# Products with gathered V rows in tiles of 32 columns, four tokens side by side

## The reference, cut to what matters

```
def gathered_attention(q, k_sel, v_sel, valid):
    logits = jnp.einsum('thd,tkhd->thk', q, k_sel).astype(jnp.float32) * (HEAD_DIM ** -0.5)
    logits = jnp.where(valid[:, None, :], logits, -jnp.inf)
    p = jax.nn.softmax(logits, axis=-1).astype(v_sel.dtype)
    return jnp.einsum('thk,tkhd->thd', p, v_sel)
```

## Time and profile before

| | |
|---|---|
| median of the runs | 1961.01 us |
| the profiled execution's own time | 1973.61 us |
| its span | 1971.5 us |
| mean granted TensorE clock | 0.905 |
| PE busy | 1653.0 us (84%) |
| DVE busy | 1057.1 us (54%) |
| ACT busy | 441.1 us (22%) |
| POOL busy | 582.4 us (30%) |

### The profile page before, as it was taken

The page is one execution under the profiler, slowest core; times in us unless marked ns, Lnnn a source line. Parts: engine busy times, 40 slices in busy tenths (PEclk is TensorE's granted clock), DMA queues, the critical chain, the costliest instruction groups (busy, mean ns, idle before and its releaser), DMA issues.

```text
span 1971.5 us, 23185 instructions
## 1 busy us (share of the span) xinstructions
PE 1653.0 (84%) x8977; PEld 1295.0 (66%) x8977; DVE 1057.1 (54%) x1778; ACT 441.1 (22%) x681; POOL 582.4 (30%) x435
## 2 busy tenths in 40 slices
PE   4875899889999699946966957776787999999998
PEld 1222388668888476846863532222786999999998
DVE  0516099988652338384888977842544333333223
ACT  2311322112112333211212320002112333322110
POOL 4001034324433222316775527774500000000000
PEclk8997999889999888988985569999898999999999
DMA  9894023222222122315997725664321222222222
GB/s 254 301 350 153 9 78 99 70 73 88 86 86 81 40 81 63 84 50 197 350 309 237 227 68 166 175 196 151 112 75 43 75 80 80 85 85 74 76 80 85
DMA packets 156032, 249.85 MB, mean 127 GB/s; under 512 B 11431, under 2 KB 104359, under 8 KB 155693
## 3 DMA queue, kind: packets, MB, share of 16 engines
q1 hardware_dynamic: 129296, 160.13, 25.6%
q0 software_dynamic: 24592, 81.40, 13.5%
q10 hardware_dynamic: 2069, 7.34, 1.1%
HBM read 238.39 MB, written 10.79 MB: 126 GB/s over the span
## 4 chain that ended last, share of the span: by engine, by line
PE 60%; DVE 19%; DMA 7%; POOL 7%; issue 4%; ACT 3%; SPq 0%; DVEq 0%; ACTq 0%; POOLq 0%
PE ps L410 32%; PE ps L452 12%; POOL kv L1964 6%; DVE EQ L1509 3%; DMA ring<-w_ffn_in 3%; PE ps L575 2%; DVE G L1739 2%; DVE kprod L1736 2%; PE ps L440 1%; PE ps L737 1%; PE ps L739 1%; PE ps L738 1%; PE ps L794 1%; PE ps L713 1%; DMA ring<-w_ffn_out 1%
## 5 line engine op out<-in xcount | busy, mean ns | idle before, releaser
L1880 POOL TENSOR_TENSOR w_lo<-w_raw,w_hi 128x1024 fp32r<-128x1024 f32 (+1 forms) x106 | 252.9, 2388 | 468.6 <-ACT w_hi L916 468.5
L916 ACT ACTIVATE w_hi<-w_raw 128x1024 fp32r<-128x1024 f32 (+1 forms) x192 | 198.4, 1034 | 803.4 <-PE ps L410 389.1
L410 PE MATMUL ps<-h_hi,w_hi 128*128 128x288 f32 x1088 | 236.8, 300 | 65.4 <-POOL w_lo L1880 25.6
L1230 DVE TENSOR_TENSOR w_lo<-w_raw,w_hi 128x1024 fp32r<-128x1024 f32 x86 | 103.2, 1201 | 271.5 <-ACT w_hi L916 265.4
L410 PE MATMUL ps<-h_lo,w_hi 128*128 128x288 f32 x1088 | 234.7, 298 | 0.0
L410 PE MATMUL ps<-h_hi,w_lo 128*128 128x288 f32 x1088 | 234.5, 297 | 0.0
L410 PEld LDWEIGHTS ps<-h_hi,w_hi 128*128 128x128 f32 x1088 | 177.1, 191 | 69.5 <-issue 23.4
L410 PEld LDWEIGHTS ps<-h_lo,w_hi 128*128 128x128 f32 x1088 | 177.3, 191 | 0.0
L410 PEld LDWEIGHTS ps<-h_hi,w_lo 128*128 128x128 f32 x1088 | 177.0, 191 | 0.0
L853 PE MATMUL ps<-kv,zq 128*128 128x512 f32 x256 | 131.3, 645 | 39.0 <-DMA kv<-cache_v,idxT 37.1
L1964 POOL DMA_INDIRECT kv<-cache_k,idxT x128 | 136.0, 1063 | 79.8 <-DVE kprod L1736 52.1
(11 more groups left out here) (427 smaller groups left out, 2873.1 us busy)
## 6 DMA issues: line engine op xcount, KB each, us to landing
w_raw<-w_ffn_in SPq DMA_DIRECT2D x88, 512.0 KB, 3.5
ring<-w_ffn_in SPq DMA_DIRECT2D x44, 512.0 KB, 7.8
w_raw<-w_ffn_out SPq DMA_DIRECT2D x40, 512.0 KB, 3.4
w_raw<-w_in SPq DMA_DIRECT2D x36, 512.0 KB, 3.7
qb<-q_scratch SPq DMA_DIRECT2D x64, 256.0 KB, 4.9
ring<-w_ffn_out SPq DMA_DIRECT2D x22, 512.0 KB, 6.9
ring<-w_in SPq DMA_DIRECT2D x12, 512.0 KB, 6.2
gate_scratch<-sgb ACTq DMA_DIRECT2D x8, 576.0 KB, 6.5
```

What stands on the lines that cost most here:

```text
L410: mm = pe.matmul(ps[:, 4 * half + 2 * m + hf_, 0:HALF], w[:, k, m * P:(m + 1) * P], x[:, kc0 + k, hf_ * HALF:(hf_ + 1) * HALF], start=(fir ...
L916: act.activation(w_hi[:, slot, 0:n], w_raw[:, slot, 0:n], ACT.Copy).then_inc(S_("hi_ready"), 1)
L1230: dve.tensor_tensor(w_lo[:, slot, 0:n], w_raw[:, slot, 0:n], w_hi[:, slot, 0:n].bitcast(F32), ALU.subtract)\
L1880: pool.tensor_tensor(w_lo[:, slot, 0:n], w_raw[:, slot, 0:n], w_hi[:, slot, 0:n].bitcast(F32), ALU.subtract)\
```

## The change

PE takes the tokens of a group in four rounds of four. The 128 output columns are divided into four tiles of 32. In round r, token a of the four goes into tile a (PSUM partitions 32a to 32a + 31), with its 8 live columns at 8r within the tile. In a round PE first issues the first half (c=0) of all four tokens, each behind the waits for its rows and its zq, and then the second half of all four; `pv_used` is added to after each token's second half. Loops over tokens are written out on PE and ACT. So that partition 8t of the bank still belongs to token t of the group, POOL and ACT take the tokens in the order that `value_token` gives: buffer a holds in round r the token 4a + r of the group. K is gathered in the old order. The number of DMAs, of products and of buffers stays the same.

```diff
+        def value_token(n):
+
+            return 16 * (n // 16) + 4 * (n % 4) + n % 16 // 4
...
-            with pe.Fori(0, 4) as g:
-                for qi in range(16):
-                    j = qi % 4
-                    pe.wait_ge(S_(f"kv_in{j}"), 32 * (16 + 4 * g + qi // 4 + 1))
-                    pe.wait_ge(S_("zq_ready"), 16 * g + (qi + 1))
-                    if qi == 0:
+            for g in range(4):
+                for r in range(4):
+                    if r == 0:
                         pe.wait_ge(S_("mz_ready"), g + 1)
                     for c in range(2):
-                        mm = pe.matmul(ps[:, 0, :], zq[:, j, c, 120 - 8 * qi:248 - 8 * qi], kv[:, j, c, :],
-                                       start=(qi == 0 and c == 0), stop=(qi == 15 and c == 1))
-                    mm.then_inc(S_("pv_used"), 1)
+                        for a in range(4):
+                            if c == 0:
+                                pe.wait_ge(S_(f"kv_in{a}"), 32 * (16 + 4 * g + r + 1))
+                                pe.wait_ge(S_("zq_ready"), 16 * g + 4 * r + a + 1)
+                            mm = pe.matmul(ps[32 * a:32 * a + 32, 0, :], zq[:, a, c, 24 - 8 * r:56 - 8 * r], kv[:, a, c, :],
+                                           start=(r == 0 and c == 0), stop=(r == 3 and c == 1))
+                            if c == 1:
+                                mm.then_inc(S_("pv_used"), 1)
                 pe.wait_ge(S_("mz_ready"), g + 2)
                 for hp in range(KA):
-                    mm = pe.matmul(ps[:, 4, bass.ds(16 * g + hp * NS, 16)], mz[:, hp * P:(hp + 1) * P], qsel[:, :],
+                    mm = pe.matmul(ps[:, 4, hp * NS + 16 * g:hp * NS + 16 * g + 16], mz[:, hp * P:(hp + 1) * P], qsel[:, :],
                                    start=True, stop=True, skip_group_check=True)
...
-            with act.Fori(0, NS // 4) as i:
-                for j in range(4):
-
-                    act.wait_ge(S_("pv_used"), 4 * i + (j + 1))
-                    act.activation(zq[:, j, :, 120:128], pT[:, :, :, bass.ds(4 * i + j, 1)].rearrange("p c h o -> p c (h o)"), ACT.Copy)\
-                        .then_inc(S_("zq_ready"), 1)
+            for n in range(NS):
+                act.wait_ge(S_("pv_used"), n + 1)
+                act.activation(zq[:, n % 4, :, 24:32], pT[:, :, :, value_token(n)], ACT.Copy).then_inc(S_("zq_ready"), 1)
...
                     for c in range(2):
-                        pool.indirect_dma_start(kv[:, n % 4, c, :], None, rows, bass.IndirectOffsetOnAxis(ap=idxT[:, c, n:n + 1], axis=0))\
+                        t = value_token(n) if w else n
+                        pool.indirect_dma_start(kv[:, n % 4, c, :], None, rows, bass.IndirectOffsetOnAxis(ap=idxT[:, c, t:t + 1], axis=0))\
                             .then_inc(S_(f"kv_in{n % 4}"), 16)
```

## The result

The changed kernel takes 2022.62 us (median of 4 runs, 2018.65 to 2029.04); the kernel before, beside it, 1961.45 us (1959.59 to 1963.5). The ratio is 1.0315, 95% interval 1.0286 to 1.0344: 61 us slower. The profiled execution has a span of 2026.9 us, 55.4 more than before, and a mean granted clock of 0.866 instead of 0.905.

The account below looks back on a forecast made before the run. POOL's issue of V gathers was taken as the bound; with buffers released together, issue, landing and release add up each round: 237.6 us to PE's end, +65.5, +3 after, 1961 + 68 = 2029 us, range 2006 to 2050.

Parts of the forecast that it names:

- What bounds: V stage: POOL's issue of gathers sets the pace, 2.5 to 2.8 us per token against PE's 1.98, landing hidden.
- The order on PE: V rounds: no buffer is free until token 3 lands, so issue 8.75, landing 3.78 and release add up each round.
- R and E: PE's release after a round's last landing, R, 2.1 us, and the whole last burst, E, 3.76 us, at the low clock.
- rival A: V stage: the clock stays high, R 1.2 and E 1.9, +51, 2012 us; chance 0.28, including a partly high clock.
- Landing: V gathers: the last DMA of a round lands 3.78 us on the mean after its issue begins, no longer covered.
- The clock: PE in the V stage: drops to 1.2 GHz, granted about 0.5 to 0.6, as PE idles about 4 us each round.
- Edits worth nothing: Written-out loops, other token order, narrower weight loads and the turn at a group's end: 0 each, with small bounds.
- After the stage: Work following PE's end, mz, L858 and two sums of L866, slower at the low clock: +3 us (0 to 8).
- DVE's last wait: DVE's wait for the last group's mz: about 100 us instead of 39.7, its taps hidden in both kernels.
- The pack's period: POOL's V issues come in sixteen packs of eight, period near 15 to 17 us; otherwise the forecast is wrong.
- Rival B: PE's pieces in different tiles don't overlap: R 3.7, E 9.3 at the low clock, 2058 us; chance 0.12.
- Rival C: Not slower: PE's time per token decides and POOL's waits of 2.5 us vanish, 1958 to 1961 us; chance 0.03.

Follow-up runs that it names:

- Experiments 6 to 8: More V buffers: 6, changed kernel with eight, ratio 0.9948; 7, kernel before with eight, 0.9955; 8, changed kernel with twelve, filled earlier, 0.9916.
- experiment 1: The changed kernel with both halves of each token multiplied together, so each token gives back its buffer when done: 1964.47 us, ratio 1.0005 to the kernel before.
- experiment 2: The changed kernel with full-width products of 128 columns, the new order of halves kept: 2053.74 us, ratio 1.0455 to the kernel before.
- experiment 5: The changed kernel with PE's waits filled by unread products, except in the first round: 2012.36 us, ratio 1.0253 to the kernel before.

## Why the prediction was right

The forecast was 2029 us, range 2006 to 2050; measured 2022.62, 61 us of loss where 68 were forecast. Point by point, by its sum from first refill to last product (measured values from the chain of waits and POOL's timeline of after):

| term | forecast | measured |
|---|---|---|
| 105 intervals at 1.25 | 131.3 | 131.3 |
| DVE beside POOL | 11 | 9.2 (105 x 0.088) |
| 15 landings | 56.7 | 58.9 |
| 15 x landing to PE | 1.8 | 0.6 |
| 14 releases R | 29.4 | 24.8 |
| 14 x PE's end to POOL | 3.6 | 2.4 |
| last burst E | 3.8 | 3.1 |
| sum | 237.6 | 230.3 |

- *What bounds:* right. POOL's issue with hidden landings is the stage's pace in the kernel before. Experiments 6 to 8, in which POOL can issue more ahead, make the time shorter, 6 and 7 by the same 9 us whatever PE's order and tiles.
- *The order on PE:* right, and shown by experiments 1 and 2: the order alone makes the loss, and taking it back alone removes it.
- *R and E:* 2.03 us for R (2.1 forecast) in nine of 14 rounds, 1.89 in one, and 1.16 in four, where the clock was high for a while (rival A's 1.2). This mix is the largest difference in the sum, 4.6 us.
- *Landing:* mean 3.93 instead of 3.78; thirteen lay between 3.55 and 3.80, and two took 5.17 and 5.67. These two hide part of what the other terms were too long by.
- *The clock:* the level was right, 0.52 to 0.70, but what takes it wasn't shown. The forecast named the idle stretch of about 4 us in each round and the quarter-width pieces. Quarter width alone isn't it: in experiment 1 such pieces ran at 1.00. Neither is needed: experiment 2 had 0.69 with full-width products and no rest over 2.7 us, and the changed kernel with eight buffers 0.73 and 0.62 with no rest over 1.9 us, where the kernel before has rests up to 1.7 us and 0.97. Where PE's waits were filled (5), the clock came back, but the filling changed the rests, the width and the amount of work at once. What of the new order costs the clock stays open. The Trainium skill (TensorE: Matmul & The Clock Gate, Part 1: The HAM clock gate) says that activity releases the throttle. The filled run agrees; the window 1100 to 1110 of the earlier trace rows, where PE was busy for all 10.00 us at 0.50, doesn't show it.
- *Edits worth nothing:* right, 1.0005 for all of them together.
- *After the stage:* +3 was forecast. The first sums of L872 took 4.13 as before, the second 5.84 instead of 4.15: +1.7.
- *DVE's last wait:* a miss without a price. About 100 us were forecast for the wait of the last mz, and it is 58.6. Of the four groups the last two stand behind the taps, and DVE waited for the third first (27.1 us); the taps themselves ended later, as the waits for the first two groups grew (19.4 and 23.3 us instead of 10.4 and 7.9). They still hide.
- *The pack's period:* 15.3 us on the mean, as forecast, single ones from 13.7 to 17.5.
- *Rival A* came true in four of 14 rounds; as a whole it would have been some 12 us less (experiment 5), where 17 were given. *Rival B* is out: eight instructions in 2.03 us do overlap; experiment 2, where they can't, shows 3.79 for its 3.7. *Rival C* would need hidden landings: with eight buffers they are, and even then the side-by-side products gain nothing over the old ones (0.9948 and 0.9955), because in both POOL's issue is what the stage runs at.

The timed difference, 61 us, is 3 above the stage's 58.2 in the profiles; the changed kernel's runs spread over 10 us, those of the kernel before over 4.

## What to carry to other kernels

Batching work over all the buffers of a ring turns the ring into a single buffer: nothing is free until the last has landed, and every round pays a landing and a release. Before regrouping a consumer, compare the turn of what is given back together (its own issues + landing + release) with the producer's time to issue the whole ring once; here two of four buffers given back together just fitted, and all four cost 3%. And a faster consumer is worth nothing where the producer's issue sets the pace; more buffers, filled earlier, were.

## What the runs showed of the hardware

- Four float32 products in tiles of 32 columns really run side by side when each has its own rows: 16 instructions in 3.64 us at the low clock (1179.24 in the trace of after) and in 1.92 at the high one, against 1.98 for 4 instructions of one full-width token.
- PE kept 2.4 GHz with a single quarter-width tile at work and rests up to 1.8 us (experiment 1, from 1190 on). It was granted 0.52 to 0.70 in the changed kernel, where most rounds have a rest of 3.3 to 4.4 us, but also 0.69 with full-width products and rests up to 2.7 us (experiment 2) and 0.62 with rests up to 1.9 us (eight buffers). Neither the width of the products nor the longest rest sorts these runs by their clock.
- An indirect DMA of 256 KB holds POOL for 0.94 to 0.95 us, with 0.30 between; with DVE at work single ones take 1.15 to 1.5 us. In both kernels with separate release and without the taps 124 of 126 intervals were 1.25 us.
- A buffer's release can reach POOL and ACT over 5 us after the products that give it have ended by the trace: 5.6 to 6.2 us in four places of the kernel before without taps, and 7 us in one of the changed kernel with eight buffers, which has no loop over tokens on PE or ACT. The cause is open.
